# Branch B's rotary in a diffusion backbone kernel: the sine product before the rotation

## What is computed

```python
def rope_1d(x, pos):
    ...
    x1, x2 = xf[..., :d // 2], xf[..., d // 2:]
    return jnp.concatenate([x1 * cos - x2 * sin, x2 * cos + x1 * sin], axis=-1).astype(x.dtype)

qb = rope(heads(px['b_q'], H_B)).reshape(B, T, KV_B, g_b, DH)
kb = rope(heads(px['b_k'], KV_B))
```

## Time and profile before

| | us |
|---|---|
| median of 3 runs | 1767.24 |
| lowest and highest | 1766.83, 1771.62 |
| profiled execution, whole time | 1772.52 |
| its span, first to last instruction | 1770.7 |
| TensorE busy | 1692.8 (96%) |
| TensorE weight loads | 1437.7 (81%) |
| VectorE busy | 1196.5 (68%) |
| ScalarE busy | 857.5 (48%) |
| GpSimd busy | 591.4 (33%) |

### The profile page before, as it was taken

The page is one execution under the profiler, slowest core; times in us unless marked ns, Lnnn a source line. Parts: engine busy times, 40 slices in busy tenths (PEclk is TensorE's granted clock), DMA queues, the critical chain, the costliest instruction groups (busy, mean ns, idle before and its releaser), DMA issues. The chain is left out here.

```text
span 1770.7 us, 29418 instructions
## 1 busy us (share of the span) xinstructions
PE 1692.8 (96%) x9657; PEld 1437.7 (81%) x9657; DVE 1196.5 (68%) x2291; ACT 857.5 (48%) x1830; POOL 591.4 (33%) x549
## 2 busy tenths in 40 slices
PE   6899999999999999899999999889999999989998
PEld 3678888788778778788888888778898888989997
DVE  4457588788778866558788664568675468756655
ACT  4456555444434443452222222667565555555444
POOL 0345634555455553111111000224435655311100
PEclk9999999999999999999999999999999999999999
DMA  8333333444433335335456764544453433546664
GB/s 284 77 73 68 84 92 90 99 123 127 117 90 102 84 78 173 101 104 147 143 165 197 232 199 128 57 106 108 102 131 98 106 74 96 162 136 178 181 203 161
DMA packets 373281, 224.67 MB, mean 127 GB/s; under 512 B 88662, under 2 KB 351244, under 8 KB 373132
## 3 DMA queue, kind: packets, MB, share of 16 engines
q1 hardware_dynamic: 363724, 216.48, 44.6%
q10 hardware_dynamic: 9408, 6.32, 1.4%
HBM read 221.65 MB, written 1.07 MB: 126 GB/s over the span
## 5 line engine op out<-in xcount | busy, mean ns | idle before, releaser
L2230 PE MATMUL bank<-Uhi,w_ring 128*128 128x512 f32 (+1 forms) x1536 | 544.8, 355 | 9.9 <-ACT under L1867 5.1
L2232 PE MATMUL bank<-Uhi,w_ring 128*128 128x512 f32 (+1 forms) x1536 | 529.7, 345 | 0.0
L2231 PE MATMUL bank<-Ulo,w_ring 128*128 128x512 f32 (+1 forms) x1536 | 529.3, 345 | 0.0
L1715 ACT ACTIVATE w_ring<-load_ring 128x512 fp32r<-128x512 f32 (+3 forms) x626 | 370.6, 613 | 177.8 <-PE bank L2232 122.2
L1948 DVE TENSOR_TENSOR w_ring<-load_ring,w_ring 128x512 fp32r<-128x512 f32 (+1 forms) x424 | 314.1, 756 | 149.4 <-ACT w_ring L1715 125.5
L2230 PEld LDWEIGHTS bank<-Uhi,w_ring 128*128 128x128 f32 x1536 | 292.7, 191 | 49.6 <-ACT under L1867 6.8
L2232 PEld LDWEIGHTS bank<-Uhi,w_ring 128*128 128x128 f32 x1536 | 292.2, 190 | 36.0
L2231 PEld LDWEIGHTS bank<-Ulo,w_ring 128*128 128x128 f32 x1536 | 293.1, 191 | 30.1
L1670 POOL TENSOR_TENSOR w_ring<-load_ring,w_ring 128x512 fp32r<-128x512 f32 (+3 forms) x202 | 251.2, 1249 | 179.8 <-ACT w_ring L1715 101.2
L1658 POOL TENSOR_TENSOR Y<-Y,small 128x512 f32<-128x512 f32 x160 | 169.3, 1058 | 320.5 <-DVE small L2172 306.7
L1837 ACT ACTIVATE Y<-bank,small 128x512 f32<-128x512 f32 (+1 forms) x192 | 117.7, 615 | 153.7 <-DVE small L2147 112.2
(11 more groups left out here) (154 smaller groups left out, 2428.6 us busy)
## 6 DMA issues: line engine op xcount, KB each, us to landing
load_ring<-in_w_in SPq DMA_DIRECT2D x192, 256.0 KB, 3.0
load_ring<-in_w_ffn_in SPq DMA_DIRECT2D x160, 256.0 KB, 3.1
mod_ring<-in_w_mod SPq DMA_DIRECT2D x96, 256.0 KB, 3.1
load_ring<-in_w_ffn_out SPq DMA_DIRECT2D x88, 256.0 KB, 3.2
mod_place<-in_w_mod SPq DMA_DIRECT2D x64, 256.0 KB, 2.8
load_ring<-in_w_branch SPq DMA_DIRECT2D x48, 256.0 KB, 2.8
mod_w<-in_w_mod SPq DMA_DIRECT2D x16, 512.0 KB, 9.5
load_ring<-in_w_in SPq DMA_DIRECT2D x64, 128.0 KB, 2.5
```

The lines of the kernel that those rows point to most:

```text
L1715: act.activation(w_ring[:, plan.slot['w', key], 0, 0:sz], load_ring[:, plan.slot['load', key], 0:sz], ACT.Copy).then_inc(sem['w_hi'], 1)
L2230: pe.matmul(dst, lhs[0], rhs[0], start=start, stop=False)
L2231: pe.matmul(dst, lhs[0], rhs[1], start=False, stop=False)
L2232: return pe.matmul(dst, lhs[1], rhs[0], start=False, stop=stop)
```

## The change

For branch B alone, the sine product is made from the projection's own bank, ahead of the rotation. VectorE's `ropeB` writes bank times sine to `tmp` after `raw_ready`. GpSimd's `ropeB` multiplies `raw` by the cosine in place, also after `raw_ready`. TensorE's `rotB` rotates `tmp` into a second bank, after `rope_sin`. VectorE's `rotB` adds that bank to `raw`. `ropeB` stands in the list right behind `evac`, `rotB` where `rot` stood; neither has an offset. The projection's bank is now freed by `raw_ready` and `rope_sin`, the rotation's by `roped`, and the `tmp` tile by the rotation. Branch D keeps the old steps.

```diff
+        'rot': ('rotated',), 'rotB': ('rotatedB',), ...
+        'ropeB': ('rope_sin',), 'rotB': ('roped',), ...
-        if kind == 'rot':
+        if kind in ('rot', 'rotB'):
             return 4 * SEQ
 ...
                 p.step('evac', key, rows=(0, rows), n=n)
+                if kind == 'B':
+                    p.take('tmp', ('rope', key), ('rotatedB', key))
+                    p.step('ropeB', key)
 ...
+                if kind == 'B':
+                    p.take('acc', ('rot', key), ('roped', key))
+                    p.step('rotB', key)
                     return
                 p.take('acc', ('rot', key), ('rope_sin', key))
 ...
+            def turned(k):
+                return [('rope_sin', k)] if b == 'B' else []
 ...
+                elif kind == 'ropeB':      (GpSimd)
+                    pool.wait_ge(sem['raw_ready'], count['raw_ready', key])
+                    pool.tensor_tensor(raw(key)[:, 0:SEQ], raw(key)[:, 0:SEQ], const('cosB'), ALU.mult).then_inc(sem['rope_cos'], 1)
 ...
+                elif kind == 'ropeB':      (VectorE)
+                    dve.wait_ge(sem['raw_ready'], count['raw_ready', key])
+                    for name, k_ in plan.freed['tmp', ('rope', key)]:
+                        dve.wait_ge(sem[name], count[name, k_])
+                    dve.tensor_tensor(tmp[:, plan.slot['tmp', ('rope', key)], 0:SEQ], acc(key)[:, 0:SEQ], const('sinB'),
+                                      ALU.mult).then_inc(sem['rope_sin'], 1)
+                elif kind == 'rotB':
+                    dve.wait_ge(sem['rotatedB'], count['rotatedB', key])
+                    dve.wait_ge(sem['rope_cos'], count['rope_cos', key])
+                    dve.tensor_tensor(raw(key)[:, 0:SEQ], acc(('rot', key))[:, 0:SEQ], raw(key)[:, 0:SEQ], ALU.add)\
+                        .then_inc(sem['roped'], 1)
 ...
+                elif kind == 'rotB':       (TensorE)
+                    for name, k_ in plan.freed['acc', ('rot', key)]:
+                        pe.wait_ge(sem[name], count[name, k_])
+                    pe.wait_ge(sem['rope_sin'], count['rope_sin', key])
+                    pe.matmul(acc(('rot', key))[:, 0:SEQ], const('rotB'), tmp[:, plan.slot['tmp', ('rope', key)], 0:SEQ],
+                              start=True, stop=True).then_inc(sem['rotatedB'], 1)
```

More of the change, by code:

```diff
@@ L112 @@
         'yend': ('y_done',), 'warm': (), 'modsum': ('mod_sum',), 'ut': ('u_turned',), 'stat': ('stat_sum',), 'bcast': ('rstd_bcast',),
-        'rot': ('rotated',), 'vtr': ('v_turned',), 'sc': ('scores',), 'sc2': ('scores',), 'second': ('scores',),
+        'rot': ('rotated',), 'rotB': ('rotatedB',), 'vtr': ('v_turned',), 'sc': ('scores',), 'sc2': ('scores',), 'second': ('scores',),
         'tr': ('p_turned',), 'pv': ('pv_done',), 'va_a': ('va_done',), 'va_b': ('piece_used',)},
@@ L125 @@
         'yg': ('y_scaled',), 'ysum': ('y_first',), 'ystat': ('y_mean',), 'hn': ('h_new',), 'hsum': ('h_first',), 'hstat': ('h_mean',),
-        'un_a': ('un_left',), 'un_b': ('un_right',), 'apB': ('ap_lo',), 'gn': ('normed',), 'rope': ('rope_sin',), 'ropeadd': ('roped',), 'ropeA': ('rope_sin',), 'ropeaddA': ('roped',),
+        'un_a': ('un_left',), 'un_b': ('un_right',), 'apB': ('ap_lo',), 'gn': ('normed',), 'rope': ('rope_sin',), 'ropeadd': ('roped',), 'ropeB': ('rope_sin',), 'rotB': ('roped',), 'ropeA': ('rope_sin',), 'ropeaddA': ('roped',),
         'qks': ('op_lo',), 'vs': ('v_lo',), 'vas': ('va_lo',), 'bias': ('bias_full',), 'mx': ('min_ready',), 'mxB': ('min_ready',),
@@ L130 @@
     'pool': {
-        'stat': ('stat_rstd',), 'mstat': ('stat_rstd',), 'ystat': ('y_rstd',), 'hstat': ('h_rstd',), 'rope': ('rope_cos',), 'ropeA': ('rope_cos',),
+        'stat': ('stat_rstd',), 'mstat': ('stat_rstd',), 'ystat': ('y_rstd',), 'hstat': ('h_rstd',), 'rope': ('rope_cos',), 'ropeA': ('rope_cos',), 'ropeB': ('rope_cos',),
         'bias': ('bias_lo',), 'den': ('prob_ready',), 'split': ('w_lo_pool',), 'gacc': ('gate_acc',), 'fh': ('hid_lo',)},
@@ L582, in rotate @@
                     p.step('ropeA', key)
+                    return
+                if kind == 'B':
+                    p.take('acc', ('rot', key), ('roped', key))
+                    p.step('rotB', key)
                     return
@@ L644, in projection @@
             qkey, nkey, vkey = ((l, b, x, j) for x in 'qkv')
+            def turned(k):
+                return [('rope_sin', k)] if b == 'B' else []
             qs = chain(qkey, b, nq, lambda: proj(low + '_q', qkey, nq, c0=j * P, halves=halves,
-                                                 frees=[(done, qkey)]), 'Q', u, qfree, g=(l, 83))
+                                                 frees=[(done, qkey)] + turned(qkey)), 'Q', u, qfree, g=(l, 83))
             if gen != u and j:
                 return qs
-            ks = chain(nkey, b, NTOK, lambda: proj(low + '_k', nkey, NTOK, c0=own, frees=[(done, nkey)]),
+            ks = chain(nkey, b, NTOK, lambda: proj(low + '_k', nkey, NTOK, c0=own, frees=[(done, nkey)] + turned(nkey)),
                        'K', gen, kfree, g=(l, 84))
@@ L1639, in _ @@
                     pool.tensor_tensor(raw(key)[:, 0:SEQ], raw(key)[:, 0:SEQ], const('cosB'), ALU.mult).then_inc(sem['rope_cos'], 1)
+                elif kind == 'ropeB':
+                    pool.wait_ge(sem['raw_ready'], count['raw_ready', key])
+                    pool.tensor_tensor(raw(key)[:, 0:SEQ], raw(key)[:, 0:SEQ], const('cosB'), ALU.mult).then_inc(sem['rope_cos'], 1)
                 elif kind == 'ropeA':
```

## The result

| | before | changed |
|---|---|---|
| median of 13 runs each, us | 1768.36 | 1773.34 |
| lowest and highest, us | 1764.13, 1772.71 | 1769.31, 1776.72 |
| ratio, 95% interval | | 1.0024 [1.0015, 1.0033] |
| span of the profiled execution, us | 1770.7 | 1771.8 |
| TensorE busy, us | 1692.8 | 1688.5 |

The changed kernel is slower by 0.24%, about 4.2 us (the two medians differ by 5.0 us). Forecast was +0.3 us, and 1773.34 us lies above the range of 1764.0 to 1771.5 us. The ratio is within the 0.3% that the prediction counts as no change, but the time isn't the one forecast. The spans of the two profiled executions hide the loss: that of the kernel before held more time at the low clock (0.985 against 0.989), and later executions of it had spans of 1764.6 to 1766.6 us.

What follows compares the result with a forecast made beforehand. TensorE, busy 96% of the span, was taken as the bound, so only its idle time counts. Losses of 2.40 us less gains of 2.10 gave +0.30 us on 1767.24, forecast 1767.5 us, range 1764.0 to 1771.5.

Steps and rivals of the forecast that it cites:

- Losses at three rotations: Layer 0's first and second and layer 1's first query: rotation waits for VectorE's sine product, +0.59, +0.87, +0.94 us.
- Second query, the two waits swallowed: Layer 0: TensorE arrives 0.87 us later at two score matmuls, so their waits of 0.24 and 0.47 us go, -0.71 us.
- Third query, -0.26: Layer 0: GpSimd's cosine product moves to the copy, so a transpose's 0.26 us wait for the normalization goes.
- Rival A: Losses come but gains don't, as something beside VectorE, such as GpSimd's weight splits, sets the chains: +1.7, 1768.9 us, chance 0.20.
- The next use of either comes behind the new waits in every one of the ten, so I cost that at nothing: All ten rotations: holding the projection's and rotation's banks longer delays no next user, cost zero.
- Fourth query, -0.79 of the 1.23 us wait: Layer 0: one-column add falls to about 0.15 us (-0.45) and the product leaves the chain (-0.34), shortening TensorE's wait.
- Layer 1's second query, -0.34: The old product leaves its place before the row minimum, whose chain ends in TensorE's 0.37 us wait: -0.34 us.
- FFN, branches A, C and D and the first 200 us aren't touched: Outside branch B TensorE is bound by itself, so the shift neither grows nor vanishes there.
- The base: The forecast sum was added to 1767.24 us, the median of three runs of the kernel before.

Runs made afterwards that it cites:

- product_early: Changed kernel with the queries' sine product earlier in VectorE's queue, 1.5 us in layer 0 and 0.5 us for layer 1's first query: 1770.67 us, ratio 1.0004.
- product_early_q3: Changed kernel with the sine product 1.5 us earlier in VectorE's queue for layer 0's fourth query alone: 1772.36 us, ratio 1.0016.
- first_old_early: Changed kernel with keys and first queries in the old order and layer 0's other queries' sine product 1.5 us earlier: 1771.51 us, ratio 1.0013.
- before_again: The kernel before, unaltered, run once more as a control for a second trace: 1768.04 us, ratio 0.9999.

## Why the prediction was wrong

**Losses at three rotations: right.** Forecast 0.59, 0.94 and 0.87 us, the steps in the shift are 0.59, 0.87 and 0.83. In layer 0 the first query's product stands behind the key's sum, as said (beside the earlier trace rows):
```profile
213.89 0.60 ACT L1803 ACTIVATE Y<-bank 128x512 f32<-128x512 f32 x1 [3.06 <-PE bank L2258]
...
214.32 0.43 DVE L2122 TENSOR_TENSOR Y<-bank,Y 128x256 f32<-128x256 f32 x1 [3.82 <-PE bank L2439]
...
214.66 0.41 DVE L2117 TENSOR_TENSOR tmp<-bank,C 128x256 f32<-128x256 f32 x1
...
215.19 0.30 PEld L2439 LDWEIGHTS bank<-tmp,C 128*128 128x128 f32 x2 [0.71 <-ACT Y L1803]
```
At the second query it stands behind the minimum with the sink (beside the earlier trace rows), and in layer 1 behind the key's sum and a reciprocal (beside the earlier trace rows):
```profile
239.54 0.21 DVE L2180 TENSOR_SCALAR small<-small,neg_sink 128x1 f32<-128x1 f32 x1
239.68 0.41 DVE L2117 TENSOR_TENSOR tmp<-bank,C 128x256 f32<-128x256 f32 x1
...
240.21 0.30 PEld L2439 LDWEIGHTS bank<-tmp,C 128*128 128x128 f32 x2 [0.82 <-issue]
```
```profile
1252.96 0.42 DVE L2122 TENSOR_TENSOR Y<-bank,Y 128x256 f32<-128x256 f32 x1 [1.17 <-PE bank L2439]
1253.30 0.15 DVE L2198 RECIPROCAL small<-small 128x1 f32<-128x1 f32 x1
1253.37 0.41 DVE L2117 TENSOR_TENSOR tmp<-bank,C 128x256 f32<-128x256 f32 x1
...
1253.89 0.30 PEld L2439 LDWEIGHTS bank<-tmp,C 128*128 128x128 f32 x2 [1.37 <-ACT Y L1803]
```

**Second query, the two waits swallowed: right.** Forecast -0.71, measured about -0.3 and -0.54. Both score groups start with no wait where the earlier trace rows has 0.24 and 0.47 us:
```profile
245.38 0.98 PE L2486 MATMUL bank<-Z 64*128 64x256 f32 x12
```
```profile
254.78 0.96 PE L2486 MATMUL bank<-Z 64*128 64x512 f32 x6
```

**Third query, -0.26: wrong, +0.57.** The step looked only at GpSimd. The sine product now stands ahead of four multiply-adds, and the one-column sum behind them (L2188, L2162 before) comes at 271.91, not just ahead of GpSimd's weight split but inside it:
```profile
269.87 0.41 DVE L2117 TENSOR_TENSOR tmp<-bank,C 128x256 f32<-128x256 f32 x1
...
270.20 1.79 DVE L1983 SCALAR_TENSOR_TENSOR mod_sums<-mod_place,sc,mod_sums 128x256 f32<-128x256 f32 x4
...
271.60 1.54 POOL L1684 TENSOR_TENSOR w_ring<-load_ring,w_ring 128x512 fp32r<-128x512 f32 x1 [2.21 <-PE bank L2521]
...
271.91 1.25 DVE L2188 TENSOR_TENSOR small<-small 128x1 f32<-128x1 f32 x1
...
274.69 0.63 PE L2521 MATMUL bank<-C,Y 128*128 128x128 f32 x4 [0.30 <-POOL Y L1672]
275.82 0.98 PE L2486 MATMUL bank<-Z 64*128 64x256 f32 x12 [0.50 <-ACT Y L1851]
```
It takes 1.25 us, and minimum, exponential and scores behind it are late. The wait of 0.26 us that was to go is still there, 0.30 us at 274.69. In product_early the same instruction is back ahead of the split and short, and the stretch gives -0.33 us, the gain that was forecast:
```profile
269.70 0.15 DVE L2190 TENSOR_TENSOR small<-small 128x1 f32<-128x1 f32 x1
269.73 1.29 POOL L1686 TENSOR_TENSOR w_ring<-load_ring,w_ring 128x512 fp32r<-128x512 f32 x1 [2.55 <-PE bank L2523]
```
Rival A had named such a stretch, and I priced it as a lost gain and not as a loss. The trace of the kernel before has the full price, a one-column sum beside a GpSimd split at 1347 us that the prediction didn't use:
```profile
1347.62 1.19 DVE L2162 TENSOR_TENSOR small<-small 128x1 f32<-128x1 f32 x1
```
The Trainium skill (SBUF — State Buffer, section on the two separate sides) has VectorE and GpSimd exclude each other there. The trace agrees, and shows it for an instruction of one column too: the sum ends at 273.16 us, the split at 273.14.

**"The next use of either comes behind the new waits in every one of the ten, so I cost that at nothing": wrong, +1.3.** This is the largest missed term in branch B. An up-projection takes the bank of layer 0's fourth query, and in TensorE's order it stands ahead of the rotation, not behind. It waited for ScalarE's copy of that bank, and now for the sine product, which is behind a minimum:
```profile
300.23 0.21 DVE L2180 TENSOR_SCALAR small<-small,neg_sink 128x1 f32<-128x1 f32 x1
300.36 0.41 DVE L2117 TENSOR_TENSOR tmp<-bank,C 128x256 f32<-128x256 f32 x1
...
300.87 0.47 PE L2256 MATMUL bank<-Z,w_ring 128*128 128x512 f32 x1 [1.08 <-issue]
...
302.66 0.30 PEld L2439 LDWEIGHTS bank<-tmp,C 128*128 128x128 f32 x2
```
The rotation at 302.66 has its room, as forecast, but the matmul 1.8 us ahead of it has none. In product_early_q3 the product is in front of the minimum, and the wait falls to 0.24 us:
```profile
300.50 0.42 DVE L2119 TENSOR_TENSOR tmp<-bank,C 128x256 f32<-128x256 f32 x1
...
301.03 0.47 PE L2258 MATMUL bank<-Z,w_ring 128*128 128x512 f32 x1 [0.24 <-issue]
```

**Fourth query, -0.79 of the 1.23 us wait: mechanism right, size off.** The one-column add is back at 0.15 us, the stretch gives -1.19 and the wait is 0.31 us (beside the earlier trace rows). As TensorE came 1.3 us later, a part was swallowed and not won; in first_old_early, later by only 0.49 us, it was still -1.01.
```profile
302.65 0.15 DVE L2188 TENSOR_TENSOR small<-small 128x1 f32<-128x1 f32 x1
...
317.63 0.96 PE L2486 MATMUL bank<-Z 64*128 64x512 f32 x6 [0.31 <-ACT Y L1851]
```

**Layer 1's second query, -0.34: right**, measured -0.34.

**"FFN, branches A, C and D and the first 200 us aren't touched": wrong for branch C.** No instruction there moved, but a fetch of TensorE's instructions did, into the first table's transfer, and the table came 1.0 to 2.0 us later in the four traces of the changed order without an early table. No row of the trace before pointed to it. That the fetch is the cause is inferred, and why it moved is open.

**The base.** I added the sum to 1767.24, the median of three runs. That of thirteen is 1768.36, 1.1 us more. Branch B 1.9, table about 1.5, base 1.1 and, outside the span, 0.14 us (time less span is 1.97 us in the mean of the changed kernel's runs, 1.83 in the kernel before) make 4.6 of the 1773.34 - 1767.24 = 6.1 us. Branch B alone, 1769.1 us, would have stayed in the range; the other terms put the time above it. The rest isn't settled. A part may be the clock: three kernels of exactly the changed order had a mean granted clock lower by 0.0002, 0.0002 and 0.0022 than the kernel before of their series, which is 0.2, 0.2 and 2.5 us at the fitted slope, but the control before_again was lower by 0.0003 too.

Forecast and rivals all had one sum of known steps. None of the four was what happened: A's 1.7 us came nearest to branch B's 1.9, by another path.

## What to carry to other kernels

When a buffer is held longer, look up for every next taker where it stands in the waiting engine's order, not where the step that frees it stands: here one of ten was ahead, and at 1.3 us it cost more than any single loss that was costed (0.94). An instruction moved by 0.3 us on a full VectorE can push a small one into a GpSimd instruction, so look at what each follower will overlap. And before differences of some us are explained, take several traces of each kernel: a single pair here mixed three causes, and the first trace of the kernel before was 4 to 6 us longer than the next ones.

## What was not expected of the hardware

- A one-column VectorE sum took 1.25 us beside a GpSimd subtraction where it takes 0.15 alone, eight times as long. The kernel before has one of 1.19 us too.
- One fetch of instructions (16 KB on queue 8) inside a 192 KB table transfer: the table was used 2.45 to 2.57 us after the fetch began in seven traces of seven, up to 1.9 us later than without. That the one causes the other is inferred. Its place was one of 1492, 1527 to 1530 and 1558 to 1568 matmuls, by kernel, and changed with VectorE's order while TensorE's stayed the same. Why is open.
- In the first 80 us the same work took up to 4.9 us more, in either kernel; the loss goes with where the stretches at 1.2 GHz fell against it.
